# Two engines' order of work inside the attention loops: TensorE turns probabilities ahead of fed work, ScalarE evicts the turn ahead of its exponentials and copies a gate ahead of a lead

## The reference

```python
def adaln(cond, w_ada, b_ada):
    m = jax.nn.silu(cond) @ w_ada + b_ada
    return jnp.split(m, 6, axis=-1)
...
def dense_attention(q, k, v, sink=None):
    s = gqa_logits(q, k)
    ...
    p = jax.nn.softmax(s, axis=-1)[..., :-1]
    return gqa_combine(p, v)
...
    yc = yc.reshape(bsz, seq, C_WIDTH) * jax.nn.silu(c_g)
    gates = jax.nn.sigmoid(m_g).reshape(bsz, seq, N_BRANCH, D_MODEL)
    merged = (gates[:, :, 0] * (ya @ w_br_a)
              + gates[:, :, 1] * (yb @ w_br_b)
              + gates[:, :, 2] * (yc @ w_br_c))
    return x + merged @ w_out
```

## Time and profile before

| | us |
|---|---|
| median of 3 runs | 1718.6 (1718.52 to 1725.3) |
| the profiled execution, its own time | 1716.63 |
| its span in the trace | 1714.8 |
| PE busy in the span | 1568.3 (91%) |
| DVE, ACT, POOL busy | 940.0, 666.3, 302.3 |
| `att1` of layer 0, from its first logits to its last values | 124.1 to 265.5 |
| `att1` of layer 1 | 764.5 to 848 |
| `att2` of layers 0 and 1 | 1216 to 1340.5, 1529.5 to 1654 |

### The profile page before, as it was taken

The page is one execution under the profiler, slowest core; times in us unless marked ns, Lnnn a source line. Parts: engine busy times, 40 slices in busy tenths (PEclk is TensorE's granted clock), DMA queues, the critical chain, the costliest instruction groups (busy, mean ns, idle before and its releaser), DMA issues.

```text
span 1714.8 us, 23566 instructions
## 1 busy us (share of the span) xinstructions
PE 1568.3 (91%) x9394; PEld 1282.9 (75%) x9394; DVE 940.0 (55%) x1316; ACT 666.3 (39%) x979; POOL 302.3 (18%) x238
## 2 busy tenths in 40 slices
PE   5999979899999999799889999699989989998997
PEld 1774547888888888674679998589878868897886
DVE  2633442554544456734456667678633667873355
ACT  2334441522222222434443333544435544454454
POOL 0214440100000000205400000121134201203331
PEclk8899989999999999899999999899999999999999
DMA  8312881132223332317645554455413444552242
GB/s 333 121 49 99 295 237 58 50 122 91 87 94 98 98 99 79 116 51 280 162 127 192 179 189 148 149 169 182 157 54 121 136 139 163 162 182 78 95 131 91
DMA packets 168672, 234.19 MB, mean 137 GB/s; under 512 B 8929, under 2 KB 116481, under 8 KB 168449
## 3 DMA queue, kind: packets, MB, share of 16 engines
q1 hardware_dynamic: 168576, 232.86, 42.0%
HBM read 231.79 MB, written 1.05 MB: 136 GB/s over the span
## 4 chain that ended last, share of the span: by engine, by line
PE 71%; DVE 7%; ACT 7%; POOL 3%; issue 2%; DMA 1%; POOLq 0%; ACTq 0%; DVEq 0%
PE psum L627 20%; PE psum L629 19%; PE psum L628 19%; PE psum L829 3%; PE psum L862 2%; DVE wl L1419 2%; PE psum L644 2%; PE psum L849 2%; ACT wh L1121 2%; PE psum L834 1%; ACT scr L1108 1%; ACT scr L1105 1%; ACT work L1200 1%; POOL work L2007 1%; DVE roped L1594 1%
## 5 line engine op out<-in xcount | busy, mean ns | idle before, releaser
L1419 DVE TENSOR_TENSOR wl<-raw,wh 128x2048 fp32r<-128x2048 f32 (+1 forms) x170 | 387.8, 2281 | 271.3 <-ACT wh L1310 151.0
L627 PE MATMUL psum<-hTh,wh 128*128 128x256 f32 (+1 forms) x1376 | 429.9, 312 | 29.4 <-ACT gates L1252 8.9
L629 PE MATMUL psum<-hTh,wl 128*128 128x256 f32 (+1 forms) x1376 | 426.3, 310 | 0.0
L628 PE MATMUL psum<-hTl,wh 128*128 128x256 f32 (+1 forms) x1376 | 426.1, 310 | 0.0
L627 PEld LDWEIGHTS psum<-hTh,wh 128*128 128x128 f32 x1376 | 265.0, 193 | 48.4 <-issue 28.5
L628 PEld LDWEIGHTS psum<-hTl,wh 128*128 128x128 f32 x1376 | 265.5, 193 | 12.9
L629 PEld LDWEIGHTS psum<-hTh,wl 128*128 128x128 f32 x1376 | 265.4, 193 | 12.5
L2007 POOL TENSOR_SCALAR work<-work,share 128x512 f32<-128x512 f32 (+4 forms) x136 | 191.5, 1420 | 395.7 <-DVE share L1644 395.7
L1310 ACT ACTIVATE wh<-raw 128x2048 fp32r<-128x2048 f32 x62 | 118.9, 1918 | 364.4 <-PE psum L629 364.4
L1121 ACT ACTIVATE wh<-raw 128x2048 fp32r<-128x2048 f32 (+2 forms) x108 | 202.8, 1877 | 137.2 <-PE psum L629 125.8
L627 PE MATMUL psum<-wh,hTh 128*128 128x512 f32 (+3 forms) x576 | 221.3, 384 | 11.4 <-DVE hTl L1490 6.9
(11 more groups left out here) (156 smaller groups left out, 1789.3 us busy)
## 6 DMA issues: line engine op xcount, KB each, us to landing
raw<-in_w_in SPq DMA_DIRECT2D x54, 1024.0 KB, 4.9
raw<-in_w_ada SPq DMA_DIRECT2D x48, 1024.0 KB, 6.5
raw<-in_w_gate SPq DMA_DIRECT2D x22, 1024.0 KB, 5.1
raw<-in_w_up SPq DMA_DIRECT2D x22, 1024.0 KB, 5.1
raw<-in_w_down SPq DMA_DIRECT2D x22, 1024.0 KB, 4.8
raw<-in_w_in SPq DMA_DIRECT2D x16, 768.0 KB, 4.3
raw<-in_w_out SPq DMA_DIRECT2D x8, 1024.0 KB, 4.9
raw<-in_w_out SPq DMA_DIRECT2D x16, 384.0 KB, 7.5
```

The lines of the kernel that those rows point to most:

```text
L627: pe.matmul(o, left[0], right[0], start=first, stop=False)
L628: pe.matmul(o, left[0], right[1], start=False, stop=False)
L629: return pe.matmul(o, left[1], right[0], start=False, stop=last)
L1419: dve.tensor_tensor(wl[:, w % SPLIT, 0:m], raw[:, u % RING, 0:m], wh[:, w % SPLIT, 0:m].bitcast(F32), ALU.subtract).then_inc(lo_ready, 1)
```

## The change

TensorE's step becomes: logits of i, turn of i-2, slot one, values of i-3, slot two. ScalarE's becomes: eviction of the turn of i-2, exponentials of i, copy of the gate if its last half was made in slot one, lead, copy of the gate otherwise (only the last, behind step 18), split.

```diff
@@ TensorE, attention @@
                         logits(steps[i])
-                    next(beside, None)
                     if 0 <= i - 2 < len(steps):
                         turn_probs(steps[i - 2])
+                    next(beside, None)
                     if 0 <= i - 3 < len(steps):
                         values(steps[i - 3])
                     next(beside, None)
@@ ScalarE, attention @@
+                def keep_gate():
+                    nonlocal gate
+                    act.wait_ge(group_done, c.next(group_done))
+                    act.activation(mgate[gate], ps[BESIDE], ACT.Copy).then_inc(evac_act, 1)
+                    gate += 1
+                    n_used[0] += 1
...
-                    turned_first = i < len(steps) and steps[i]["score_after"] == 2
-                    if turned_first:
+                    if 0 <= i - 2 < len(steps):
                         keep_turned(i - 2)
                     if i < len(steps):
                         probs(i)
+                    if second and HALF_GATES[min(i, 18)][0] and sum(map(sum, HALF_GATES[0:i])) % 2:
+                        keep_gate()
                     if i < n_four:
                         four_evacuated()
-                    if 0 <= i - 2 < len(steps) and not turned_first:
-                        keep_turned(i - 2)
                     if 0 <= i - behind < len(steps):
                         lead(i - behind)
                     if i < n_four:
                         four_led(i)
                     if second and GATES_BY[min(i, 18)] - (i == 18) > gate:
-                        act.wait_ge(group_done, c.next(group_done))
-                        act.activation(mgate[gate], ps[BESIDE], ACT.Copy).then_inc(evac_act, 1)
-                        gate += 1
-                        n_used[0] += 1
+                        keep_gate()
```

## The result

| | before | changed |
|---|---|---|
| median of 5 runs each, us | 1719.05 (1718.52 to 1726.52) | 1705.20 (1702.87 to 1706.89) |
| the profiled execution, us | 1716.63 | 1706.89 |
| its span, us | 1714.8 | 1705.1 |
| mean granted clock of TensorE | 0.965 | 0.972 |

The ratio is 0.9924, with a 95% interval of 0.9897 to 0.9951: the change makes the kernel 0.8% faster. The forecast of 1713.5 (a ratio of 0.997) was 8.3 us too slow. Its range (1701 to 1725) holds the time; the case that it called likeliest, no measurable change, did not come.

The account below looks back on a forecast made before the run. TensorE's work was taken as the floor of the attention stages, its idle time as what order can change. -24.0 us (second model) + 18.9 (first) = -5.1: profiled 1711.5, plus 2.0 to the median, 1713.5 us; range 1701 to 1725.

Parts of the forecast that it names:

- The gate copy: Second model's attention: TensorE's waits for ScalarE's copy fall from 10.1 to about 1.5 us in each stage.
- step 2: Second model's attention: the turn of step 0 waits for POOL, 1.2 us idle where 1.4 stood.
- step 7: Second model's attention: of the 3.02 us gap before the gate's copy, some 0.75 us remain.
- step 8: Second model's attention: no wait for the copy, but the next gate's weight split on VectorE holds TensorE some 0.65 us.
- a slow half: Second model's attention: with gaps so short no half at low clock was expected, 2 x 1.5 = 3.0 us won per stage.
- POOL beside the split: Second model's attention: POOL's scaling takes 3.50 us beside VectorE's weight split, 1.82 alone, so the turn just doesn't wait.
- The remainder's wait in `att1`: First model's attention: values wait longer for VectorE's remainder, 6.5 us lost in the longer stage, 3.3 in the shorter.
- The turn's wait for POOL: First model's attention, steps with fed work: the turn waits for POOL's scaling, 6.6 us lost in the longer stage, 6.3 shorter.
- The rival by which it waits less: First model's attention: the turn waits less for POOL; without those 12.9 us the time is 1700.6; chance 0.15.
- some 1.5 us of low clock behind it: First model's longer stage: low clock behind the 2.4 us wait for w_ada's loads goes, some 1.5 us won back.
- 0 for the tails: First model's tails without fed work: ScalarE waits up to 0.7 us for a turn, hidden by the late next share: 0.
- The clock rival: First model's attention: idle gaps lower TensorE's clock, 1.5 us in each of eleven step pairs, 16.5 us, 1730.0; chance 0.10.

Follow-up runs that it names:

- second profile: The changed kernel measured once more, nothing altered, beside the kernel before: 1705.92 us, ratio 0.9927.
- second-only kernel: Against the changed kernel, TensorE's and ScalarE's new order kept in the second model's attention only, the first model's as before: 1698.49 us, ratio 0.9897.
- the one with TensorE's order only: Against the kernel before, only TensorE's new order, in the second model's attention only, ScalarE everywhere as before: 1697.44 us, ratio 0.9895.
- first-only kernel: Against the changed kernel, the new order kept in the first model's attention only, the second model's as before: 1733.16 us, ratio 1.0092.
- the one with ScalarE's order only: Against the kernel before, only ScalarE's new order, in the second model's attention only, TensorE everywhere as before: 1725.48 us, ratio 1.0044.

## Why the prediction was right and wrong, point by point

- **The gate copy: right.** The waits fell to 0.9 us for a forecast of 1.5, the stages to 112.7 for 112.5. The places were step 2 (1.13 found, 1.2 forecast), step 7 (0.93 and 0.75) and step 8 (0.41 and 0.65); not foreseen were 0.99 us for POOL in step 16. Idle won was 8.3 us (forecast 9.0), clock 3.5 (forecast 3.0). The 1.5 us of a slow half in that forecast are the two windows of the earlier trace rows, 4.48 us busy against 3.03; before, the last stage has two such spells, with matmuls of 0.41 us where others of the same form take 0.28 (1586.0 to 1589.0 and 1603.2 to 1605.4), and the changed stages read 1.00. That both engines' moves carry it was wrong in emphasis: TensorE's alone gives 10.5 of 11.9.
- **POOL beside the split: the sum by the row was near, but not for the one late turn.** The sum rested on 3.50 us and had turns just in time. Waits of turns for POOL in the second `att2` stage are 2.1 us; forecast by the row were 1.2, so the excess is 0.9 us. It is the one late turn, which waits 0.99 us and shows nearly a whole split on top:

```profile
1632.64 2.27 DVE L1422 TENSOR_TENSOR wl<-raw,wh 128x2048 fp32r<-128x2048 f32 x1
1632.82 4.35 POOL L2010 TENSOR_SCALAR work<-work,share 128x128 f32<-128x128 f32 x3 [3.28 <-DVE share L1647]
1636.33 0.44 PE L849 MATMUL psum<-ident,work 128*128 128x128 f32 x2 [0.99 <-POOL work L2010]
```

  POOL began 0.18 us into the split of 2.27 us, and the first instruction of its row took 2.88 us, where that form takes 0.60 with no split beside it. In the earlier trace rows POOL began 0.26 us ahead of the split; its first instruction took 1.02 us, and the second, of the same form (0.92 alone), 2.50. So in these two places what was added, 1.6 us there and 2.3 here, is about what was left of the split when that POOL instruction began, 1.7 us and 2.1, and I had taken one price for all. The split itself took 2.45 us in the earlier trace rows, against 2.29 alone, though 0.76 us of POOL's first instruction were left when it began: it lost 0.16 us, less than POOL did.
- **The remainder's wait in `att1`: right.** +6.7 us (3.7 to 10.4) and +3.1 (1.5 to 4.6), forecast 6.5 and 3.3; one gap 1.59 for 1.66.
- **The turn's wait for POOL: right.** 5.8 and 5.7 us, forecast 6.6 and 6.3. The rival by which it waits less would have given 1700.6, nearer to the measured 1705.2 than my 1713.5, and it isn't the reason.
- **What missed: the low clock in the longer stage.** The waits there are right, so the miss is in two terms of the sum, "some 1.5 us of low clock behind it" and 0 for the tails. Idle time in the fed part rose by 9.8 us, against 6.5 + 6.6 - 2.4 - 0.6 = 10.1. But busy time fell by 3.4 us with fed work and by 2.0 in the tail, 5.4 where I had 1.5. Before, the clock of the fed part read so:

```profile
124.10:130.00 5.90, 5.21 (x10) 1.96 (x11) 1.40 (x2) 2.98 (x6) 0.00 (x0) 0.71 0.00 0
130.00:234.00 104.00, 94.37 (x707) 48.88 (x706) 44.98 (x106) 41.56 (x115) 44.52 (x32) 1.00 0.63 220
234.00:237.60 3.60, 3.02 (x18) 2.00 (x18) 1.18 (x3) 0.60 (x1) 1.82 (x2) 0.55 1.07 221
```

  The last window, behind the wait for w_ada, is the spell that I had: 3.60 us at 0.55 cost some 1.6 us (an estimate, length times what the clock lacks). The first, 5.90 us at 0.71, cost some 1.7 us by the same estimate, stands at the stage's very start, and was in no term. The changed kernel's profile has 1.00 there, but its second profile has 0.71 over the same 5.90 us. So this part was luck of one execution. The tail's clock varies too, from 0.70 to 0.86 over the last 27 to 29 us of the stage in eight of the profiles. With before's order in that stage four kernels took 142.52, 140.52, 141.37 and 146.82 us, at mean clocks of TensorE from 0.91 to 0.95 and with 2.4, 4.1, 4.1 and 5.4 us of waits for w_ada; with the new order it took 146.47, 147.11 and 146.89. By means of these (142.8 and 146.8) the stage loses 4.0 us, so 3.95 is in line with the other executions and 8.5 was probably too much; a single profile of the stage is uncertain by some 3 us. The shorter stage, at clock 1.00 in its fed part both times, cost 9.34 for 10.4.
- **From trace to median.** I set the profiled execution 2.0 us under its median, as it was before. The changed kernel's lies 1.7 above. These 3.7 us and the 4.6 us by which the profiled times differ from the forecast (1706.9 for 1711.5) are the whole 8.3. The 4.6 are the 5.4 of the stages less the 0.8 us by which the rest grew. The 3.7 belong to no mechanism of the prediction.
- **The clock rival: refuted, but not for the reason given against it.** Granted clock is 1.00 in both fed parts, though TensorE is idle for 20.7 of 119.9 and 14.5 of 73.7 us there. The argument was that the half right behind the longest gap ran at 1.00. That is so in the last stage only. In the other `att2` stage of the same trace, the half behind the same gap of 3.02 us (TensorE alone; the same columns as the earlier trace rows) had this:

```profile
1260.30:1263.60 3.30, 3.01 (x18) 0.72 0.00 0
```

  So one gap was followed by a low clock in one stage and by the full clock in its twin, and that slow half had no second gap of 2 or 3 us near it. In the last stage the full clock of 1.00 stood behind a gap of 3.02 us, and the slow half of the earlier trace rows, at 0.62, behind one of 1.92: the length of a gap alone does not tell these apart.

## What to carry to other kernels

When an engine's work is moved, look at what the engines it waits for have queued ahead of the instruction that it now needs sooner. Here VectorE waited for the fed sums with the share and the remainder queued behind that wait; moving them ahead gave 17 us more than the changed kernel, and nothing for it had to be added. An order change in a loop that two models share should be tried in each alone: here the stages of one gained 24 us and those of the other lost 13, and only the difference shows in the whole.

## What the runs showed of the hardware that was not expected

In a stretch that no edit touches, the same waits were followed by different clocks in different kernels. These are two windows each, behind the same wait of 5.0 us for ScalarE (line 714), of the second-only kernel and of the one with TensorE's order only:

```profile
1385.00:1405.00 20.00, 19.18 (x78) 16.13 (x77) 14.32 (x20) 9.67 (x13) 2.99 (x2) 0.79 0.44 140
1405.00:1425.00 20.00, 18.16 (x82) 15.39 (x81) 9.88 (x14) 8.14 (x9) 0.00 (x0) 0.91 0.45 135
```

```profile
1391.00:1411.00 20.00, 18.98 (x85) 15.84 (x84) 16.09 (x26) 9.66 (x13) 3.10 (x2) 0.91 0.44 140
1411.00:1431.00 20.00, 18.68 (x90) 15.71 (x89) 11.61 (x11) 9.17 (x11) 2.00 (x1) 1.00 0.53 162
```

Up to the windows TensorE's waits in that stretch agree within 0.01 us in the two kernels. It has the same work there and finished the stretch in 192.52 us in the one and 188.94 in the other. The first-only kernel took 192.83 us, the one with ScalarE's order only 190.58, the six others 188.5 to 189.0. On a kernel of 1700 us one such spell is 0.2%, so a term of less than about 4 us can't be read from one profiled execution unless its own waits are. Against that, gaps of 1.3 to 1.6 us, once or twice in every two steps of `att1`, and 17 and 20% of idle time in all, left the granted clock at 1.00. What tells the two cases apart was not tried.
